# Five orders changed in a one-core encoder block: the small vectors, the token sums, the exchange of operands, and the first tiles of down

## The reference

```python
h  = rms_norm(x, norm1_g);  proj = h @ w_in          # q 512 | k 128 | v 128 | p 512
a  = sliding_window_sink_attention(q, k, v, sinks)   # chunks of 64, own chunk and the one before
m  = multiscale_pool(p, pool_w, pool_b, pool_scale)  # trailing means over 2, 4, 8, 16
x  = x + concat([a, m]) @ w_out
u  = rms_norm(x, norm2_g) @ w_up                     # 2 * 2816 columns
c  = causal depthwise conv of width 3 over u, plus conv_b
x  = x + (silu(c_gate) * c_value) @ w_down           # 2816 -> 1024
```

## Time and profile before

| | |
|---|---|
| median of 3 runs | 1829.86 us (1827.72 to 1835.39) |
| profiled execution | 1829.45 us |
| its span | 1827.6 us |
| PE busy | 1769.4 us (97% of the span) |
| DVE busy | 1360.2 us (74%) |
| ACT busy | 836.2 us (46%) |
| POOL busy | 251.4 us (14%) |
| mean granted TensorE clock | 0.990 |
| chain that ended last | PE 82%, DVE 7%, ACT 4%, issue 3%, DMA 2% |

### The profile page before, as it was taken

The page is one execution under the profiler, slowest core; times in us unless marked ns, Lnnn a source line. Parts: engine busy times, 40 slices in busy tenths (PEclk is TensorE's granted clock), DMA queues, the critical chain, the costliest instruction groups (busy, mean ns, idle before and its releaser), DMA issues.

```text
span 1827.6 us, 23467 instructions
## 1 busy us (share of the span) xinstructions
PE 1769.4 (97%) x8490; PEld 1471.9 (81%) x8490; DVE 1360.2 (74%) x1818; ACT 836.2 (46%) x1467; POOL 251.4 (14%) x278
## 2 busy tenths in 40 slices
PE   7899999999988999999999999999997999999999
PEld 6787888888877888888887888888886888888887
DVE  5665645654757999899898898898985776775774
ACT  4564554644655444444454444444443433333331
POOL 1212112201340000000000000000002122220210
PEclk9999999999999999999999999999998999999999
DMA  6242263364447332432455322323225999986984
GB/s 202 60 151 80 70 226 109 116 219 144 141 150 268 127 92 70 144 121 81 139 201 215 103 70 81 93 71 103 70 82 173 345 356 305 303 269 185 301 288 144
DMA packets 218563, 295.51 MB, mean 162 GB/s; under 512 B 12937, under 2 KB 120145, under 8 KB 218449
## 3 DMA queue, kind: packets, MB, share of 16 engines
q1 hardware_dynamic: 199280, 241.48, 41.0%
q10 hardware_dynamic: 19169, 52.54, 7.4%
HBM read 234.20 MB, written 59.77 MB: 161 GB/s over the span
## 4 chain that ended last, share of the span: by engine, by line
PE 82%; DVE 7%; ACT 4%; issue 3%; DMA 2%; POOL 1%; ACTq 0%; SPq 0%; DVEq 0%; POOLq 0%
PE ps L683 27%; PE ps L685 26%; PE ps L684 26%; ACT xs L1050 2%; DVE w_lo L1312 1%; ACT junk L962 1%; DMA rw<-in_w_up_dram 1%; DMA x_d<-r 1%; DMA vv<-h2T_d 1%; PE ps L827 1%; ACT w_hi L944 1%; DVE cb L1568 0%; PE ps L729 0%; DVE wv L1508 0%; DVE sums L1359 0%
## 5 line engine op out<-in xcount | busy, mean ns | idle before, releaser
L683 PE MATMUL ps<-va_hi,wv 128*128 128x512 f32 x1232 | 483.1, 392 | 21.1 <-DVE ub L1614 12.6
L684 PE MATMUL ps<-va_lo,wv 128*128 128x512 f32 x1232 | 482.2, 391 | 0.0
L685 PE MATMUL ps<-va_hi,wv 128*128 128x512 f32 x1232 | 481.8, 391 | 0.0
L683 PEld LDWEIGHTS ps<-va_hi,wv 128*128 128x128 f32 x1232 | 233.1, 189 | 71.2 <-issue 21.4
L685 PEld LDWEIGHTS ps<-va_hi,wv 128*128 128x128 f32 x1232 | 233.1, 189 | 48.9
L684 PEld LDWEIGHTS ps<-va_lo,wv 128*128 128x128 f32 x1232 | 233.1, 189 | 48.2
L683 PE MATMUL ps<-dt_hi,ds_hi 128*128 128x512 f32 x616 | 239.8, 389 | 0.0
L684 PE MATMUL ps<-dt_lo,ds_hi 128*128 128x512 f32 x616 | 239.6, 389 | 0.0
L685 PE MATMUL ps<-dt_hi,ds_lo 128*128 128x512 f32 x616 | 239.6, 389 | 0.0
L1568 DVE SCALAR_TENSOR_TENSOR cb<-ub,cst,cb 128x1024 f32<-128x1024 f32 x176 | 218.7, 1286 | 7.1 <-ACT cb L1155 7.1
L1155 ACT ACTIVATE cb<-ub,cst 128x1024 f32<-128x1024 f32 x88 | 109.5, 1244 | 151.4 <-DVE ub L1623 93.3
(11 more groups left out here) (169 smaller groups left out, 2874.3 us busy)
## 6 DMA issues: line engine op xcount, KB each, us to landing
dg<-gT_d SPq DMA_DIRECT2D x264, 256.0 KB, 5.0
rw<-in_w_up_dram SPq DMA_DIRECT2D x84, 512.0 KB, 5.1
dw<-in_w_down_dram SPq DMA_DIRECT2D x132, 256.0 KB, 5.3
gT_d<-cb ACTq DMA_DIRECT2D x44, 512.0 KB, 2.6
raw<-in_w_in_dram SPq DMA_DIRECT2D x40, 512.0 KB, 3.7
raw<-in_w_out_dram SPq DMA_DIRECT2D x32, 512.0 KB, 3.9
n<-in_x_dram SPq DMA_DIRECT2D x16, 512.0 KB, 5.9
vs<-h2T_d SPq DMA_DIRECT2D x16, 512.0 KB, 7.3
```

What stands on the lines that cost most here:

```text
L683: pe.matmul(out_ap, l_hi, r_hi, start=first, stop=False, skip_group_check=True)
L684: pe.matmul(out_ap, l_hi, r_lo, start=False, stop=False, skip_group_check=True)
L685: return pe.matmul(out_ap, l_lo, r_hi, start=False, stop=last, skip_group_check=True)
```

## The change

1. **Small vectors.** PE turns the first tokens of each of four tiles at once, seven column tiles (0, 1, 2, 3, 5, 6, 7), and the small vectors between the second and the third tile; column tile 4, which shares their bank, comes last. DVE copies `cst` after scaling the third tile. The first projection takes its column tiles in the same order.
2. **Token sums and halves at the step to up.** POOL makes s1 and s2 of c = 1 ahead of s3 and s4 of c = 0. `va (0, 2)` moves behind `va (1, 0)`, and `va (1, 1)` behind out-unit (1, 1). `V_ORDER` and `first_up` follow; `t13(1)` moves from ahead of `add_u3(0)` to behind the last token halves. SP's load of tile 1's weights waits for s4 of c = 1 too.
3. **Exchange.** `vv_hi` and `vv_lo` of operands 5 and 6 move from the end of tile 21 into tile 22.
4. **Loads of down's first tiles.** Weight tiles 0, 1 and 2 are all loaded ahead of the wait for the gated store.
5. **Halves of down's first tiles.** In tile 43 two weight tiles are split ahead of `add_u3` and `keep_c11`, one after them, then the three token tiles, then tiles 3 and 4 around `add_c21`.

```diff
     units("t2", last - 1, (2,), (3,))
-    units("va", last, (0, 1), (0, 2))
+    units("va", last, (0, 1))
     units("o", last, (1, 0))
-    units("va", last, (1, 0), (1, 1))
+    units("va", last, (1, 0), (0, 2))
     units("o", last, (1, 1))
-    units("va", last, (1, 2))
+    units("va", last, (1, 1), (1, 2))
     units("o", last, (1, 2), (1, 3))
...
+def t1_order(a):
+    return (0, 1, 2, 3, 5, 6, 7, 4) if a == 0 else tuple(range(KT))
...
-V_ORDER = [(0, 0), (0, 1), (0, 2), (1, 0), (1, 1), (1, 2), (0, 3), (1, 3), (0, 4), (1, 4), (0, 5), (1, 5), (1, 6), (0, 6)]
+V_ORDER = [(0, 0), (0, 1), (1, 0), (0, 2), (1, 1), (1, 2), (1, 3), (0, 3), (1, 4), (0, 4), (1, 5), (0, 5), (1, 6), (0, 6)]
...
# SP
             wait(sp, "v_lo", V_DONE[1, 4])
+            wait(sp, "s4", 2)
             load_rw(1)
...
             wait(sp, "u_lo", NP * made(N_UP))
+            for tau in range(WRAW):
+                load_t(tau)
             for i in range(-S_LEAD, N_S):
                 for tau in T_MADE[i]:
-                    load_t(tau)
+                    if tau >= WRAW:
+                        load_t(tau)
...
# PE, t1 of block 0
-                    pe.wait_ge(vectors_read, 1)
-                    for t in range(NT):
-                        pe.wait_ge(S["xs1"], t + 1)
-                        for dt in range(KT):
-                            tr = pe.transpose(ps[:, t1_bank(0, dt), tokens(t)], n1[:, t, dt * P:(dt + 1) * P], ident[:])
+                    for t in range(NT):
+                        if t == 2:
+                            vectors()
+                        pe.wait_ge(S["xs1"], t + 1)
+                        for dt in t1_order(0)[:7]:
+                            turn(dt, t)
+                    pe.wait_ge(vectors_read, 1)
+                    for t in range(NT):
+                        turn(4, t)
...
# ACT, first_up
+                v_hi(1, 3)
                 v_hi(0, 3)
-                v_hi(1, 3)
+                v_hi(1, 4)
                 keep_p1(0)
                 v_hi(0, 4)
-                v_hi(1, 4)
+                v_hi(1, 5)
                 v_hi(0, 5)
-                v_hi(1, 5)
                 keep_p5(0)
...
# ACT, up: vv_hi(5) behind keep_p1(22), vv_hi(6) behind keep_p5(22); before: behind tap2(21, 1)
                 if un == N_UP - 1:
-                    for tau in range(T_EARLY):
-                        t_hi(tau)
+                    t_hi(0)
+                    t_hi(1)
                 keep_c11(un)
...
                 if un == N_UP - 1:
+                    t_hi(2)
                     for sigma in range(S_LEAD):
                         s_hi(sigma)
+                    for tau in range(3, T_EARLY):
+                        t_hi(tau)
...
# DVE, n1_ of block 0
-                dve.wait_ge(const_turned, 1)
-                v.tensor_copy(cst[:], ps[:, 0, 0:200]).then_inc(vectors_read, 1)
-                n1sc(a)
+                for t in range(NT):
+                    scale(0, a, t, n1)
+                    if t == 2:
+                        dve.wait_ge(const_turned, 1)
+                        v.tensor_copy(cst[:], ps[:, 0, 0:200]).then_inc(vectors_read, 1)
...
# DVE, first_up
+                v_lo(1, 3)
                 v_lo(0, 3)
-                v_lo(1, 3)
+                v_lo(1, 4)
                 n2sc(NB - 1)
                 add_u2(0)
-                for i in (4, 5):
-                    v_lo(0, i)
-                    v_lo(1, i)
-                t13(1)
+                v_lo(0, 4)
+                v_lo(1, 5)
+                v_lo(0, 5)
                 add_u3(0)
                 add_c22(0)
                 v_lo(1, 6)
                 v_lo(0, 6)
+                t13(1)
...
# DVE, up: vv_lo(5) ahead of glu1(21), vv_lo(6) behind glu2(21), both ahead of add_u3(22)
                 if last:
-                    for tau in range(T_EARLY):
-                        t_lo(tau)
+                    t_lo(0)
+                    t_lo(1)
                 add_u3(un)
...
                 if last:
+                    t_lo(2)
                     for sigma in range(S_LEAD):
                         s_add(sigma)
                         s_lo(sigma)
                 add_c12(un)
+                if last:
+                    t_lo(3)
                 add_c21(un)
+                if last:
+                    for tau in range(4, T_EARLY):
+                        t_lo(tau)
...
# POOL, va
-                if i == 0:
-                    if c:
-                        s1(c)
-                    s2(c)
+                if i == 0 and c == 0:
+                    s2(0)
+                    s1(1)
+                elif i == 0:
+                    s2(1)
                 elif i == 2:
                     s34(c)
```

More of the change, by code:

```diff
@@ L704, in by_token, with vectors, turn @@
                 mm.then_inc(S["unit_used"], 1)
+            def vectors():
+                pe.wait_ge(vectors_in, VECTORS_IN)
+                pe.transpose(ps[:, 0, 0:112], vec_rows[0:112, 0, :], ident[0:112, 0:112])
+                pe.transpose(ps[:, 0, 112:200], vec_rows[0:88, 1, :], ident[0:88, 0:88]).then_inc(const_turned, 1)
             def t1(a, h):
                 if a == 0:
+                    def turn(dt, t):
+                        tr = pe.transpose(ps[:, t1_bank(0, dt), tokens(t)], n1[:, t, dt * P:(dt + 1) * P], ident[:])
+                        if t == NT - 1:
+                            tr.then_inc(S["turned1"], 1)
+                    for t in range(NT):
[4 more added lines that the diff above has]
+                            turn(dt, t)
                     pe.wait_ge(vectors_read, 1)
                     for t in range(NT):
-                        pe.wait_ge(S["xs1"], t + 1)
-                        for dt in range(KT):
-                            tr = pe.transpose(ps[:, t1_bank(0, dt), tokens(t)], n1[:, t, dt * P:(dt + 1) * P], ident[:])
-                            if t == NT - 1:
-                                tr.then_inc(S["turned1"], 1)
+                        turn(4, t)
                     return
@@ L735, in pin @@
                 w = n % RING
-                for k in range(KT):
-                    if g == 0 and k > (0 if a == 0 else 4):
-                        pe.wait_ge(S["hT_lo"], KT * a + k + 1)
+                for i, k in enumerate(t1_order(a)):
+                    if g == 0 and i > (0 if a == 0 else 4):
+                        pe.wait_ge(S["hT_lo"], KT * a + i + 1)
                     c = slice(k * P, (k + 1) * P)
                     mm = passes(ps[:, P_BANK + g, :], w_hi[:, w, c], w_lo[:, w, c], hT_hi[:, k, :], hT_lo[:, k, :],
-                                k == 0, k == KT - 1)
+                                i == 0, i == KT - 1)
                 mm.then_inc(S["unit_used"], 1)
@@ L867, in _ @@
             pe.wait_ge(const_pool, CONST_POOL)
-            pe.wait_ge(vectors_in, VECTORS_IN)
-            pe.transpose(ps[:, 0, 0:112], vec_rows[0:112, 0, :], ident[0:112, 0:112])
-            pe.transpose(ps[:, 0, 112:200], vec_rows[0:88, 1, :], ident[0:88, 0:88]).then_inc(const_turned, 1)
             walk(dict(t1=t1, pin=pin, pm=pm, kv=kv, q=q, kt=kt, qt=qt, s=s, sp=sp, av=av, o=o, t2=t2))
@@ L979, in t1 @@
                     act.wait_ge(S["unit_used"], used("q", a - 1, 3))
-                for dt in range(KT) if a == 0 else range(4 * h, 4 * h + 4):
-                    act.wait_ge(S["turned1"], KT * a + dt + 1)
+                for i in range(KT) if a == 0 else range(4 * h, 4 * h + 4):
+                    dt = t1_order(a)[i]
+                    act.wait_ge(S["turned1"], KT * a + i + 1)
                     a_.activation(hT_hi[:, dt, :], ps[:, t1_bank(a, dt), :], ACT.Copy, scale=gain[0][:, dt:dt + 1]
@@ L1213, in up @@
                 keep_p1(un)
+                if un == FT:
+                    vv_hi(5)
                 if un == FT - 1:
@@ L1221, in up @@
                 keep_p5(un)
+                if un == FT:
+                    vv_hi(6)
                 if un == FT - 1:
@@ L1237, in up @@
                 if un == N_UP - 1:
+                    t_hi(2)
                     for sigma in range(S_LEAD):
                         s_hi(sigma)
+                    for tau in range(3, T_EARLY):
+                        t_hi(tau)
                 tap2(un, 1)
-                if un == FT - 1:
-                    vv_hi(5)
-                    vv_hi(6)
             def t_hi(tau):
@@ L1342, in t1 @@
             def t1(a, h):
-                for dt in range(KT) if a == 0 else range(4 * h, 4 * h + 4):
-                    dve.wait_ge(S["hT_hi"], KT * a + dt + 1)
+                for i in range(KT) if a == 0 else range(4 * h, 4 * h + 4):
+                    dt = t1_order(a)[i]
+                    dve.wait_ge(S["hT_hi"], KT * a + i + 1)
                     v.scalar_tensor_tensor(hT_lo[:, dt, :], ps[:, t1_bank(a, dt), :], gain[0][:, dt:dt + 1],
@@ L1665, in up @@
                 t4(un + 1)
+                if un == FT:
+                    vv_lo(5)
                 glu1(un - 1)
@@ L1671, in up @@
```

(10 more changed lines are left out.)

## The result

The changed kernel takes 1813.12 us (median of 4 runs, 1811.2 to 1814.76); the kernel before took 1831.64 us in the same comparison. The ratio is 0.9899, with a 95% interval of 0.9873 to 0.9924: 18.5 us faster, just above the range of 1798 to 1812 that was given. The direction was right, the size was not: 25.4 us had been summed up.

A forecast was written before the change was run, and what follows sets the result against it. The prediction took PE, busy 97% of the span, as the bound, so only its waits and the slow clock behind them pay. 1.9 + 5.5 + 5.9 + 12.1 = 25.4 us off 1829.86 gave 1804.5 us, range 1798 to 1812.

The forecast's parts named there:

- Small vectors: At the start: token scaling begins earlier and the first projection starts 1.9 us sooner, bounds 0 and 2.7.
- Step to up: Between the first stage and up: two PE waits go, a new 4.5 us one appears; gain 5.5 us.
- The 5.2 and 4.7 us waits: PE's waits for the last out-unit's weight halves and tile 0's last token halves; both were to go.
- 522.1 + 1.1 + 2 x 1.2: At the step to up: DVE's first row addition starts at about 525.4, behind two token halves of 1.2 us each.
- rival (a): The step to up gives 1 us or less if PE's new wait is 9 us or more; 1809 to 1811, chance 0.12.
- Exchange: Up tiles 21 and 22: earlier taps leave 0.2 to 0.5 us of wait; gain 5.9 us, bounds 4 and 6.4.
- Down's first tiles: From up's last tile into down: the 11.7 us wait goes; gain 12.1 us after a 2 us charge.
- Steady up and down I cost at nothing: In the steady tiles: no instruction is added and every moved one keeps its place, so 0 us.
- the 14.1 us: Loss at up tile 43 against the beat of 19.04 us per tile, 11.7 of it wait; to be recovered.
- The charge of 2 us for tiles 5 and 8: In down: late halves at token tile 5 and again at tile 8 cost 2 us, bounds 0 and 6.
- Rival (b): PE waits at most of down's first eleven tiles, giving back 6 us or more; 1810 to 1812, chance 0.10.
- Case (d): In steady up: DVE carries its lag through 43 tiles at 0.7 us each, losing 30 us; 1834, chance 0.03.

The follow-up runs named there:

- after_sums: The changed kernel with POOL making s3 and s4 of c = 0 ahead of s1 and s2 of c = 1: 1814.16 us, ratio 0.991.
- after_adds: The changed kernel with the four row additions ahead of `v_lo(1, 2)` on DVE: 1813.96 us, ratio 0.9916.
- step_only: The kernel before with only the change to token sums and halves at the step to up: 1827.72 us against 1829.55, ratio 0.9987.
- after_taps: The changed kernel with the four convolution taps of up tile 43 spread over steps 2 to 5 of down: 1814.09 us, ratio 0.9908.
- down_only: The kernel before with only the changed loads and halves of down's first tiles: 1825.17 us against 1829.55, ratio 0.9973.

## Why the prediction was half right

**Small vectors: right.** Forecast 1.9 us, 2.1 measured at the end of the stage, 2.25 at the first `hT_lo`. DVE's subtractions set the pace, as said. No run has part 1 alone, but the end of this stage lies at 488.8 to 490.2 us in the four kernels without it and at 487.0 to 488.0 in the nine with it.

**Step to up: the mechanism was right, one term mis-sized.** The 5.2 and 4.7 us waits went, POOL waited for the fourth quarter, a new wait for the scaled rows came, and tile 1 gave something back (1.7 us for `add_u3`, 1.7 for `keep_p5`; 3.1 forecast for the first). Counted from the start of the step, PE began tile 1 5.6 us sooner (564.39 - 489.63 and 556.73 - 487.52), where 8.2 had been summed up, and tile 1 gave 2.6 of it back, where 2.2 had been. The term that failed is "522.1 + 1.1 + 2 x 1.2" for the first row addition: the two halves took 5.67 us, 3.3 more. PE's new wait became 8.0 instead of 4.5 us. The prediction had this mechanism in hand, from the Trainium skill, "SBUF — State Buffer", section "SBUF: two separate sides", and weighed it for the taps only. It holds here too: both halves read two SBUF operands, and the sums beside them read SBUF. after_sums bears it out: apart from the sums the pair takes 2.36 us, and the step is 1.9 us shorter. The port is not the whole of the miss, though: in after_adds the additions came early and the wait stayed, for the roots. The rival (a) was near: 8 us of its 9.

**Exchange: the mechanism was right, the exact number in part luck.** 5.9 us, forecast 5.9. The taps started at 964.50, right behind ACT's tap, and 0.24 us of PE's wait for `add_u3(22)` remained (0.2 to 0.5 forecast). But the stretch took 44.50, 44.25, 43.27 and 41.73 us in the four kernels without part 3, and 38.35 to 38.69 in the nine with it. In before the clock fell behind the 3.8 us wait; in step_only, at 41.73, a wait of 3.3 us kept the full clock. So part 3 is worth 3 to 6 us by execution, 4.9 in the mean. No run has it alone.

**Down's first tiles: wrong in the term "Steady up and down I cost at nothing".** The 11.7 us wait and its slow clock went. But the 14.1 us could not be kept. Data for the first 63 token tiles came at a pace that PE had met with 0.1 us to spare; PE, 14 us sooner, ran into it. By the beat, up should end 19.04 us behind `add_c21(42)`: at 1391.26 in the kernel before, and at 1380.38 in the changed one (1361.34 + 19.04). PE starts token tile 62 182.6 us later in the first (1573.86) and 178.0 us later in the second (1558.36): the data did come sooner, by 4.6 us. From there to the end both take 253.8 us. So down gained these 4.6 us and no more. after_taps shows it: with tile 5 mended PE goes on at the same 1558.4. The kernels with lighter loads show that it is bytes: 3.4 us less in down with the taps as they are (2.0 under the shortest of the four full-load kernels), 8.9 with the taps spread.

The charge of 2 us for tiles 5 and 8 was small as well: where the loads are light, spreading the taps is worth 4.2 us. `t_lo(4)` and one more of ACT's copies stood ahead of the taps, and from `add_c21(43)` to tile 5's halves it took 13.2 us (forecast 11.3). Under full loads mending it gained nothing, since the wait only came later instead of earlier. Rival (b), that down starves, was the right kind and given 0.10. It was looked for in the first eleven tiles, where room was 2 us or more, and sits near tile 62.

**Case (d)** did not occur: from `add_c21(22)` to `add_c21(42)` it is 380.80 us in the kernel before and in the changed one, and at most 381.12 in any kernel here.

The 1.1 us by which the range was missed are a third of the 3.3 us that the two halves took longer beside the sums, and a seventh of the 7.5 us that down fell short by.

## What to carry to other kernels

Before a stall is costed at its full length, ask of every stream behind it how much room its data has at the tightest place, up to the end of the kernel: tile by tile, end of the producer against start of the consumer. "PE never waits there" does not say that there is room; here a DMA share of 1.00 over 110 us went with 0.1 us of room. Where two limits lie close together, as tile 5 and the loads did here, mending one alone can gain little or nothing. And where DVE subtractions with two SBUF inputs are moved beside POOL's sums, cost both as longer: here 5.67 us in place of 2.36, and 3.38 in place of 2.39.

## What the runs showed of the hardware

- Short instructions of POOL were stretched most in proportion. The two steps of a root, on 128x1 elements, took 0.19 and 0.55 us with DVE idle beside them, and 1.25 and 1.41 beside DVE's token halves. Rows of the changed kernel, POOL:

```profile
533.05 0.19 POOL L1788 TENSOR_SCALAR rstd<-ss 128x1 f32<-128x1 f32 x1
533.33 0.55 POOL L1790 TENSOR_TENSOR rstd<-rstd,half_neg 128x1 f32<-128x1 f32 x1
533.97 1.25 POOL L1788 TENSOR_SCALAR rstd<-ss 128x1 f32<-128x1 f32 x1
535.30 1.41 POOL L1790 TENSOR_TENSOR rstd<-rstd,half_neg 128x1 f32<-128x1 f32 x1
```

- The clock behind a wait of nearly three us was not the same from run to run: in down_only a wait of 2.75 us was followed by a matmul of 0.50 us (granted clock 1.00), in after_taps one of 2.60 us by 0.79 (0.57). The row of the changed kernel behind its 2.91 us has the granted clock at 0.60, and then 0.55 (us; busy PE, PEld, DVE, ACT, POOL; clock; DMA share; GB/s):

```profile
1396.00:1400.00 4.00, 2.51 (x6) 2.02 (x7) 2.64 (x5) 1.18 (x2) 2.80 (x1) 0.60 0.41 143
1400.00:1404.00 4.00, 4.00 (x11) 3.08 (x11) 3.39 (x3) 2.21 (x4) 1.28 (x1) 0.55 0.80 250
```

- The same code took up to 2 us more or less in the first stage from one execution to the next (`add_c21(0)` at 562.47, 563.14 and 564.63 in three kernels that are alike up to there). The parts were therefore compared by stretches between landmarks, and the stretches differ too: 112.8 to 114.6 us for the step without part 2, 41.7 to 44.5 for the exchange without part 3.
